# A linear recurrence beside the q, k, v projection: its steps moved by one token tile

## The reference

```
h = rms_norm_2(x, norm_mix[layer]);  proj = h @ w_in[layer]
lru_in, lru_gate, q, k, v, ... = split(proj)
xc = causal_depthwise_conv(lru_in, conv_w, conv_b)              # 4 taps
r = sigmoid(xc @ wa + ba);  i = sigmoid(xc @ wx + bx)           # per block of 128 channels
log_a = -8 * r * softplus(-lam)
b = sqrt(-expm1(2 * log_a)) * i * xc
h_t = exp(log_a)_t * h_(t-1) + b_t                              # over the tokens
out = gelu(lru_gate) * h
```

## Time and profile before

| | |
|---|---|
| time, three runs | 4750.97, 4752.97, 4757.22 us (median 4752.97) |
| span of the profiled execution | 4752.7 us; no own time is given beside it |
| mean granted TensorE clock | 0.912 |
| TensorE busy | 84% of the span |
| VectorE, ScalarE, GpSimd busy | 58%, 43%, 10% |
| this stage | first matmul at 2672.07 us, first load of the next stage at 3044.51 us |

### The profile page before, as it was taken

The page is one execution under the profiler, slowest core; times in us unless marked ns, Lnnn a source line. Parts: engine busy times, 40 slices in busy tenths (PEclk is TensorE's granted clock), DMA queues, the critical chain, the costliest instruction groups (busy, mean ns, idle before and its releaser), DMA issues. The chain is left out here.

```text
span 4752.7 us, 76279 instructions
## 1 busy us (share of the span) xinstructions
PE 4004.5 (84%) x31217; PEld 3199.8 (67%) x31217; DVE 2760.1 (58%) x4042; ACT 2047.4 (43%) x3461; POOL 470.8 (10%) x376
## 2 busy tenths in 40 slices
PE   6999976878887675999939889699989896499994
PEld 4888744448886454888838767477777664388883
DVE  4222155566665558999951476455543354599995
ACT  3111022545553324777731344355532232377772
POOL 0000012210001200111010132000000000111111
PEclk9999966979999787999969999899999898699997
DMA  5332221652223445999942232322133304699996
GB/s 203 133 133 99 79 99 53 176 166 80 78 80 112 143 178 200 395 398 390 377 150 93 92 113 85 105 71 75 55 109 104 113 28 179 251 409 413 410 413 249
DMA packets 378959, 842.33 MB, mean 177 GB/s; under 512 B 32703, under 2 KB 249823, under 8 KB 328182
## 3 DMA queue, kind: packets, MB, share of 16 engines
q1 hardware_dynamic: 360526, 787.44, 45.2%
q0 software_dynamic: 12032, 41.96, 2.8%
q10 hardware_dynamic: 6056, 8.08, 0.5%
HBM read 673.03 MB, written 164.35 MB: 176 GB/s over the span
## 5 line engine op out<-in xcount | busy, mean ns | idle before, releaser
L506 PE MATMUL psum<-proj_hi,proj_w 128*128 128x512 f32 (+2 forms) x1728 | 461.8, 356 | 13.1 <-DVE proj_w L548 11.4
L4443 DVE TENSOR_TENSOR moe_lo<-moe_raw,moe_hi 128x2048 fp32r<-128x2048 f32 x192 | 428.4, 2286 | 33.6 <-ACT moe_hi L4398 33.6
L4398 ACT ACTIVATE moe_hi<-moe_raw 128x2048 fp32r<-128x2048 f32 x192 | 357.0, 1911 | 40.9 <-PE psum L4359 40.9
L506 PEld LDWEIGHTS psum<-proj_hi,proj_w 128*128 128x128 f32 (+1 forms) x1728 | 303.9, 188 | 66.6 <-DVE proj_w L548 11.6
L506 PE MATMUL psum<-proj_lo,proj_w 128*128 128x512 f32 (+2 forms) x864 | 306.2, 354 | 0.0
L517 DVE COPY proj_out<-psum 128x512 f32<-128x512 f32 (+3 forms) x54 | 32.5, 603 | 355.6 <-PE psum L506 355.6
L2738 DVE TENSOR_TENSOR moe_lo<-ahead_raw,moe_hi 128x2048 fp32r<-128x2048 f32 x96 | 219.1, 2290 | 23.5 <-ACT moe_hi L2686 23.4
L2738 DVE TENSOR_TENSOR moe_lo<-lT,moe_hi 128x2048 fp32r<-128x2048 f32 x96 | 218.9, 2290 | 21.9 <-ACT moe_hi L2686 21.9
L2686 ACT ACTIVATE moe_hi<-ahead_raw 128x2048 fp32r<-128x2048 f32 x96 | 184.2, 1919 | 70.9 <-PE psum L2639 70.9
L2686 ACT ACTIVATE moe_hi<-lT 128x2048 fp32r<-128x2048 f32 x96 | 183.9, 1919 | 66.3 <-PE psum L2639 66.3
L1798 DVE COPY_PREDICATED chunks_X<-chunks_msk,psum 128x128 f32<-128x128 int32 x400 | 107.8, 302 | 152.3 <-PE psum L1551 138.0
(11 more groups left out here) (647 smaller groups left out, 9940.2 us busy)
## 6 DMA issues: line engine op xcount, KB each, us to landing
moe_raw<-in_w_gate_up SPq DMA_DIRECT2D x128, 1024.0 KB, 9.6
moe_raw<-in_w_down SPq DMA_DIRECT2D x64, 1024.0 KB, 7.8
lT<-in_w_gate SPq DMA_DIRECT2D x36, 1024.0 KB, 9.3
ahead_raw<-in_w_down SPq DMA_DIRECT2D x36, 1024.0 KB, 8.0
ahead_raw<-in_w_up SPq DMA_DIRECT2D x32, 1024.0 KB, 10.1
lT<-in_w_up SPq DMA_DIRECT2D x32, 1024.0 KB, 9.7
ahead_raw<-in_w_gate SPq DMA_DIRECT2D x28, 1024.0 KB, 8.9
lT<-in_w_down SPq DMA_DIRECT2D x28, 1024.0 KB, 7.9
```

The lines of the kernel that those rows point to most:

```text
L506: ins = nc.tensor.matmul(bank[e * nch + c][0:width, 0:n], l, r, start=(k == 0 and i == 0), stop=(k == KD - 1 and i == 2))
L4398: nc.scalar.activation(hi[:, n % R], raw[:, n % RAW], ACT.Copy).then_inc(s["hi_ready"], 1)
L4443: nc.vector.tensor_tensor(lo[:, n % R], raw[:, n % RAW], hi[:, n % R], ALU.subtract).then_inc(s["lo_ready"], 1)
```

## The change: what it does

Within a block the steps move by one tile on every engine. `convolve(b)` stays at VectorE's first tile of a block (n = 3b). TensorE's gates move from the second and third tile to the first and second; ScalarE's work with them. `input_scale` moves from the third tile to the second. `gated_x` and `recur`, which were at the first tile of the next block, move to the third tile of their own. SyncE loads the gate weights of the next block after the second gate, at n = 3b + 2. No instruction is added or removed; the operations and their shapes stay.

```
--- before.py
+++ after.py
@@ -2872,9 +2872,9 @@
                     load_w(q)
                 for n in range(STEPS + 2):
                     b = n // 3
-                    if n % 3 == 0 and 0 < b < KD:
-                        sp.wait_ge(l["i_mm"], b)
-                        load_block(b, "w")
+                    if n % 3 == 2 and b + 1 < KD:
+                        sp.wait_ge(l["i_mm"], b + 1)
+                        load_block(b + 1, "w")
                     if n % 3 == 0 and b + 1 < KD:
                         sp.wait_ge(l["xc"], b + 1)
                         load_block(b + 1, "x")
@@ -2955,8 +2955,8 @@
 
                 for n in range(STEPS):
                     products(n)
-                    if n % 3:
-                        gate(n // 3, n % 3 - 1)
+                    if n % 3 < 2:
+                        gate(n // 3, n % 3)
                     if 2 <= n <= NQK + 1:
                         turn(n - 2)
 
@@ -3035,10 +3035,10 @@
                     else:
                         values(n)
                     b = n // 3
-                    if n % 3 == 1:
+                    if n % 3 == 0:
                         sigmoid(b, 0)
                         decay(b)
-                    elif n % 3 == 2:
+                    elif n % 3 == 1:
                         act.wait_ge(l["u"], b + 1)
                         nc.scalar.activation(u[:, :], u[:, :], ACT.Sqrt).then_inc(l["root"], 1)
                         sigmoid(b, 1)
@@ -3077,9 +3077,9 @@
                     pool.wait_ge(l["i"], b + 1)
                     nc.gpsimd.tensor_tensor(i_[:, :], i_[:, :], xc[:, :], ALU.mult).then_inc(l["ix"], 1)
 
-                for n in range(STEPS + 1):
-                    if n % 3 == 0 and n:
-                        gated_x(n // 3 - 1)
+                for n in range(STEPS):
+                    if n % 3 == 2:
+                        gated_x(n // 3)
                     if n < NQK:
                         rotate(n)
 
@@ -3206,15 +3206,15 @@
                         dve.wait_ge(s["tr"], n - 1)
                     V.tensor_copy(y[:, n % 2, BANK:], bank[2 * (n % 2) + 1][:, :]).then_inc(s["vD"], 1)
 
-                for n in range(STEPS + 1):
+                for n in range(STEPS):
                     b = n // 3
-                    if n % 3 == 0 and b:
-                        recur(b - 1)
+                    if n % 3 == 2:
+                        recur(b)
                     if n in (NT - 1, 2 * NT - 1):
                         rest((n + 1) // NT)
-                    if n % 3 == 0 and b < KD:
+                    if n % 3 == 0:
                         convolve(b)
-                    if n % 3 == 2:
+                    if n % 3 == 1:
                         input_scale(b)
                     if n < NQK:
                         scale(n)
```

## The result

The changed kernel took 4771.72 us in the median of 5 runs (4761.80 to 4774.98) against 4754.29 of before (5 runs, 4750.97 to 4759.27): ratio 1.0034, 95% interval 1.0022 to 1.0046. Timed again with more runs (experiment `a0_again`) it stood at 1.0024 (1.0014 to 1.0034), 4763.94 against 4754.15. The forecast was 4765, 12 us slower.

A forecast was written before the change was run, and what follows sets the result against it. TensorE was taken as the bound, except at the opening, two weight changes and the end; seven parts summed to +11.9 us, taking the span from 4752.7 to 4764.6, forecast 4765. Range 4752 to 4776; the forecast's own, 4760 to 4772.

The forecast's parts named there:

- slower by more: Rival: convolve blocked for 3.5 us instead of 2.3, or gate waits letting the clock fall: 4770 to 4776, chance 0.10.
- Part 2: Blocks 1 to 4: gates wait for a convolution that GpSimd's rotation blocks 2.3 us per block (bounds 0 and 3.5): +7.5 us.
- part 1: Opening: the first gate, now ahead of tile 1, leaves TensorE idle 11.4 us, then at half clock: +12.4 us.
- part 3: First change of weights (step 7): input_scale(2) and ScalarE's Sqrt, Sigmoid and Gelu now stand ahead of the transpose: +3.3 us.
- part 7: Tail: block 7's chain starts at tile 22's end, so the next stage's load follows TensorE by 6.1 us: -11.0 us.
- Part 5: Second change of weights (step 15): gate(5, 0) ahead of tile 16 waits for convolve(5) behind rest(2): +4.6 us.
- Part 6: Tiles of v: recur a tile earlier lets the store leave in time, and four gates are left: -6.6 us.
- part 4: Up to tile 14 TensorE has one gate more behind it: +1.7 us, given back in part 6.
- No difference that can be told: Rival: GpSimd and convolve share time without loss; sum +0.2 us, time 4753, chance 0.26.
- Faster: Rival: subtractions, not loads, pace the changed weights once rest(2) comes 11 us earlier: 4749, chance 0.09.

The follow-up runs named there:

- a0_again: The changed kernel with no edit, timed again against the kernel before: stage 383.7 us, ratio 1.0024.
- e2_port: Changed kernel, but GpSimd starts the rotation of every third tile of a block only after the next block's convolution: stage 372.3 us, ratio to before 1.0001.
- e4_last_block: Kernel before, with the change made for block 7 alone: stage 373.0 us, ratio to before 0.9998.
- e3_gate5: Changed kernel, but block 5's first gate stands behind tile 16's products, as before: stage 377.4 us, ratio to before 1.0012.
- e9_port_gate5: Changed kernel with the edits of e2_port and e3_gate5 together: stage 364.7 us, ratio to before 0.9985.
- e6_last_three: Kernel before, with blocks 5 to 7 in the new order, except block 5's first gate behind tile 16's products: stage 358.8 us, ratio to before 0.9977.
- e8_all_fixed: Changed kernel with e2_port's and e3_gate5's edits, plus tile 7 handled first behind the first new weights: stage 368.4 us, ratio to before 0.9995.

## Why the prediction was right, and where it was not

**The total.** Forecast +11.9 in the stage, measured +11.2 and +11.3 in two profiled executions, and a ratio of 1.0024 that is 11.4 us. The first five runs alone, at 4771.72, would have stood at the upper end of the forecast's own range and inside the rival "slower by more". The forecast's sign and size held, and so did each thing that was to show it: the idle time ahead of the first L2953 (10.0, forecast 11), L3153 at 2.52 (forecast "near 2.5"), 13.9 us ahead of the transpose (forecast 15), 18.3 ahead of the gate (over 15), and the load 6.3 us behind the last matmul (6). That the sum is within 0.7 is in part luck: single lines of the table miss by +2.8, -2.3 and -2.2, and the misses cancel.

**Part 2, the blocking.** It decided the forecast, +11.9 instead of +0.2, and is shown: without the overlap the stage is 11.4 us shorter (`e2_port`) and the convolution back at 4.7. It rested on one row of before, a subtraction that took 3.02 instead of 1.23. The Trainium skill (SBUF — State Buffer, section "Who interferes with whom") also counts a `tensor_scalar`, with its one SBUF input, among the operations that can take the port pair shared with GpSimd, when it runs in a 2-port mode. No row names the mode of the first pass, but its rows agree: 0.81 us alone, 2.52 beside the rotation, with its end behind the rotation's first instruction. The size of the waits was right (11.2 us in the four blocks for 11.9), that of the whole a little low: after two of the waits the clock had fallen, which the prediction had kept for its slower rival. Behind the wait of 3.21 us, gate, transpose and tile took 16.4 us (2740.27 to 2756.63) instead of 13.5. That is the +4.2 where +1.4 stood.

**Parts 1, 3 and 7, the cause.** The two ends were sized right (+13.1 for 12.4, -10.8 for -11.0); the first change of weights added 2.2 us where 4.5 stood (43.5 us for 45.7), about half of the miss because `rest(1)` took 15.5 us (2793.57 to 2809.03) and not 16.6. The reading behind parts 1 and 3 was wrong. The prediction put +12.4 on the gate's place ahead of tile 1, and the wait behind the first change on `input_scale` and ScalarE's order there. Taking either away moved the wait to the next gate (11.45 and 19.84 us) and gave 3.1 and 0.1 us. What bounds these stretches is a chain across all the engines, which the place of one instruction does not shorten: convolution, gate, Sigmoid, `input_scale`, scaling of a tile, rotation, `gated_x`, scan, scaling, next convolution. This is concluded from where the waits went, and from `e2_port`, which shortens one link of the chain and with it the waits. Between two blocks' first gates TensorE has three tiles to cover it, in the old order as in the new. At the switch from one to the other it has two, and at the opening there is one tile ahead of the first gate instead of two. So the new order pays up to one tile, some 11 us, where it begins, and gets one tile back at the end, where the last block is done a tile earlier. `e4_last_block` shows both in one: 10.57 us of wait, and a tail as short as the changed kernel's. What fails is therefore to read parts 1, 3 and 7 as separate prices, though as a sum for this kernel they hold: parts 1 and 7 are the two ends of one shift, and the wait of part 3 is the same chain, met behind the new weights.

**Part 5.** The gate's place costs what it was expected to: 6.3 us come back when it is moved (`e3_gate5`). Within the changed kernel the stretch was 2.2 us cheaper than worked out, since the granted clock was up again when the transpose behind the gate ran (transpose and tile 16 took 11.8 us, 2947.47 to 2959.27, where 1.6 + 11.4 = 13.0 stood) and `rest(2)` took 18.2 us (2921.01 to 2939.22), not 19.1. The 2.5 us put there for the rotation beside `rest(2)` do not show in the time: `e2_port` takes the rotation away, `rest(2)` is back at 16.2 us (2915.48 to 2931.72) and the gate's wait falls from 18.2 to 17.0, but gate, transpose and tile behind it take 16.4 us instead of 15.3.

**Part 6.** -7.2 for -6.6, of which 1.7 is the gate of part 4 given back, so some 5.5 us are gained; TensorE's wait of 3.3 us for a store is gone. It is not the only gain. With the losses of parts 2 and 5 taken away (`e9_port_gate5`), the changed order's stage is 7.7 us shorter than before's: the opening costs 12.3 and blocks 1 to 4 cost 3.0 (1.7 of it the gate), the tail gives 10.8, tile 17's start to the last product gives 6.2 (1.7 of it the gate), and the second change of weights gives 6.0, because `recur(4)` no longer stands ahead of `rest(2)`: that starts 7.9 us behind tile 14 (2903.30 to 2911.17) and not 18.7. The prediction had this earlier start in part 5, where the gate that waits for `convolve(5)` used it up. Started at the second change of weights, where TensorE waits anyway, the new order hardly pays for its beginning and keeps the tail's gain (`e6_last_three`, 13.6).

**The rivals.** "No difference that can be told" had the right condition and price: GpSimd and the convolution out of each other's way gives 1.0001. "Faster", by subtractions at their own pace, had nothing to it: `rest(2)` came earlier and still waited for its slices, 18.2 us for what takes 9.8 alone.

## What to carry to other kernels

To start a pipeline's steps one slot earlier shortens the end by a slot and lengthens the beginning by one; the two nearly cancel (here 12 to 13 us and 11), unless the beginning falls into a wait that is there anyway, so look for such a wait (here a change of weights) and switch there. When a wait is taken away, ask what chain ran beside it: twice here a wait of over 10 us moved to the next instruction that needed the same chain. Before an operation is moved, see what else will run at its new time on the engine that can block it; one row with an unusual duration in the old trace can price that.

## What was not expected of the hardware

The lower bound of part 2 let a pass with one SBUF input slip through. It does not: the `tensor_scalar` of 128x1024 takes 2.51 to 2.53 us instead of 0.81 in blocks 1 to 4 of the changed kernel's profile, and ends 0.56 us behind the GpSimd instruction beside it, as the subtraction with two inputs ended 1.1 us behind its own. After that the two engines slow each other by turns: VectorE's three passes took 4.41 instead of 3.93, and GpSimd's small instructions 1.58 instead of 0.75.

What a wait of 2 to 5 us ahead of a gate does to the granted clock differs from place to place and from run to run: the gate behind it took from 1.95 to 3.75 us. The 3.08 us of the earlier trace rows were followed by 3.75 us at a granted clock of 0.50 (1.2 of 2.4 GHz). Here are a gate of `e8_all_fixed`, at 1.00 (2.4 GHz), and one of `a0_again`, at 0.68, between the two levels:

```profile
2936.89 1.96 PE L2953 MATMUL psum<-qkv_xc,qkv_lw 128*128 128x512 f32 x4 [3.08 <-issue]
```

```profile
2785.56 2.76 PE L2953 MATMUL psum<-qkv_xc,qkv_lw 128*128 128x512 f32 x4 [2.42 <-issue]
```
